# Three blocks with a mixture of experts on one core: expert order from counts, last projection by row tiles, gate vector on expert outputs

## The reference

```python
mod = cond @ w_mod[l] + b_mod[l]
sh1, sc1, g1, sh2, sc2, g2 = [m[:, None, :] for m in jnp.split(mod, 6, axis=-1)]
h = _layer_norm(x) * (1 + sc1) + sh1
y = _token_mixer(h, ..., w_out[l], b_out[l])
x = _layer_norm(DEEPNORM_ALPHA * x + g1 * y, post1_g[l], post1_b[l])
h = _layer_norm(x) * (1 + sc2) + sh2
y = _moe(h, w_router[l], b_router[l], w_gu[l], b_gu[l], w_dn[l], b_dn[l])
x = _layer_norm(DEEPNORM_ALPHA * x + g2 * y, post2_g[l], post2_b[l])
```

## Time and profile before

| | |
|---|---|
| timed runs (3) | 2307.07, 2309.64, 2311.7 us; median 2309.64 |
| profiled execution | 2306.96 us, its span 2304.8 us |
| granted clock of TensorE, mean | 0.985 |
| busy share PE, PEld, DVE, ACT, POOL | 94%, 49%, 33%, 20%, 3% |
| DMA | 591.35 MB, mean 257 GB/s |

### The profile page before, as it was taken

How to read it: one execution, slowest core, us unless ns; L and a number is a source line. 1 busy time by engine, 2 the same in 40 slices (tenths; PEclk the granted TensorE clock), 3 DMA queues, 4 the chain that set the end, 5 groups by cost and what they waited for, 6 DMA issues and landing times.

```text
span 2304.8 us, 30211 instructions
## 1 busy us (share of the span) xinstructions
PE 2159.5 (94%) x11510; PEld 1133.0 (49%) x11511; DVE 752.1 (33%) x1835; ACT 464.1 (20%) x922; POOL 65.4 (3%) x79
## 2 busy tenths in 40 slices
PE   6999999989999998999989998999999999999998
PEld 5744454333333333333333334744565446787873
DVE  1795243222222122222222223231212353988100
ACT  1012111111111111111101111131112215897100
POOL 0000000000000000000000000000000000222000
PEclk9999999999999999999999999999999999999999
DMA  9654667779999999999995899435234333232241
GB/s 375 227 188 147 228 223 279 284 296 418 418 418 417 418 418 383 418 417 418 417 381 223 356 418 354 146 138 190 73 124 146 109 117 112 74 111 74 108 163 40
DMA packets 157319, 591.35 MB, mean 257 GB/s; under 512 B 5072, under 2 KB 5136, under 8 KB 124352
## 3 DMA queue, kind: packets, MB, share of 16 engines
q1 hardware_dynamic: 152240, 572.03, 63.4%
q0 software_dynamic: 4384, 16.40, 2.0%
q10 hardware_dynamic: 624, 1.93, 0.2%
HBM read 589.29 MB, written 1.05 MB: 256 GB/s over the span
## 4 chain that ended last, share of the span: by engine, by line
PE 74%; DMA 15%; DVE 5%; ACT 3%; DVEq 2%; issue 1%; SPq 0%; ACTq 0%
PE PS L609 22%; PE PS L912 14%; DMA W<-in_w_gu 13%; PE PS L597 10%; PE PS L935 6%; PE PS L1119 4%; PE PS L624 4%; PE PS L859 2%; PE PS L948 2%; PE PS L1192 1%; DVE BIG L1875 1%; PE PS L876 1%; DVE BIG L1879 1%; DMA W<-in_w_mod 1%; DVEq L1878 1%
## 5 line engine op out<-in xcount | busy, mean ns | idle before, releaser
L609 PE MATMUL PS<-W,BIG 128*128 128x512 f32 x1152 | 501.4, 596 | 5.0 <-DVE BIG L2309 2.9
L912 PE MATMUL PS<-W,BIG 128*64 128x512 f32 x2048 | 451.8, 595 | 21.2 <-DMA W<-in_w_gu 21.2
L609 PEld LDWEIGHTS PS<-W,BIG 128*128 128x128 f32 x1152 | 219.5, 191 | 277.5 <-issue 270.8
L912 PEld LDWEIGHTS PS<-W,BIG 128*64 128x64 f32 x2048 | 142.1, 137 | 313.2 <-issue 270.9
L935 PE MATMUL PS<-W,BIG 128*64 128x512 f32 x1024 | 228.9, 600 | 6.9 <-ACT BIG L1362 6.9
L597 PE MATMUL PS<-BIG,W 128*128 128x256 f32 x1024 | 222.2, 379 | 1.5 <-ACT BIG L353 1.5
L597 PEld LDWEIGHTS PS<-BIG,W 128*128 128x128 f32 x1024 | 194.2, 190 | 29.0 <-ACT BIG L353 1.9
L1873 DVE TENSOR_SCALAR BIG<-PS 128x512 f32<-128x512 f32 (+1 forms) x38 | 24.7, 650 | 382.2 <-PE PS L912 356.5
L935 PEld LDWEIGHTS PS<-W,BIG 128*64 128x64 f32 x1024 | 71.0, 138 | 143.9 <-issue 126.3
L1119 PE MATMUL PS<-BIG,W 128*128 128x256 f32 x512 | 118.4, 385 | 0.5 <-ACT BIG L1517 0.5
L1357 ACT ACTIVATE BIG<-BIG 128x512 f32<-128x512 f32 x32 | 20.2, 630 | 489.0 <-DVE BIG L1873 489.0
(11 more groups left out here) (452 smaller groups left out, 1942.6 us busy)
## 6 DMA issues: line engine op xcount, KB each, us to landing
W<-in_w_gu SPq DMA_DIRECT2D x128, 2048.0 KB, 17.6
W<-in_w_dn SPq DMA_DIRECT2D x64, 2048.0 KB, 19.2
W<-in_w_in SPq DMA_DIRECT2D x24, 2048.0 KB, 18.9
W<-in_w_mod SPq DMA_DIRECT2D x12, 2048.0 KB, 10.9
W<-in_gla_w_in SPq DMA_DIRECT2D x10, 2048.0 KB, 7.9
W<-in_s_w_in SPq DMA_DIRECT2D x8, 2048.0 KB, 9.0
W<-in_s_w_glu SPq DMA_DIRECT2D x8, 2048.0 KB, 8.6
W<-in_w_out SPq DMA_DIRECT2D x6, 2048.0 KB, 7.7
```

Source lines behind the costliest of these rows:

```text
L609: ins = pe.matmul(ps[:, t, :], lhs(i * KT + k)[:, t * P:(t + 1) * P], w[:, k, :], start=i + k == 0, stop=last_chunk and k == KT - 1)
L912: ins = pe.matmul(PS[hh[h], g, :], XET[:, k, :], gu_w(k)[:, g * D + h * CH:g * D + (h + 1) * CH], start=False, stop=k == KT - 1, skip_grou ...
```

## The change

Four things. (1) The experts are taken in an order worked out on the chip. VectorE ranks them by falling count, with expert 0 set ahead of all and smaller numbers first among equals; the place in the loop of rank r is the number whose five bits are those of r reversed. TensorE brings counts and numbers into that order with two products; `PERM` holds the expert's number for each place. SyncE loads it for the weights' addresses, VectorE at the top of each expert and once more in the branch of the extra blocks. (2) `halves_by_rows` computes row tile 0 of both halves of `w_out`, then tile 1; VectorE adds ALPHA times `X` and g1 times the bias ahead of it, and runs both norms' statistics tile by tile (`tile_scale`), as ScalarE takes the roots. (3) The product with g2 moves to each expert's output: VectorE writes `YE` as the product with `GAIN_H` (`YEX` with `GAIN_Q`) where ScalarE copied it, and `b_dn` is multiplied by g2 once. (4) ALPHA times `X` goes into the PSUM banks by a product with ALPHA times the identity (`residual_in`) in place of the zero sums; behind the loop the statistics are read from PSUM.

```diff
+    own = -np.arange(NE, dtype=np.float32)
+    own[0] = 4 * T * NE
+    c[:, C_TIE:C_TIE + NE] = own
+    c[0:NE, C_OWN] = own
+    c[0:NE, C_OWN + 1] = np.arange(NE)
+    spread = sorted(range(NE), key=lambda i: int(f"{i:05b}"[::-1], 2))
+    c[:, C_PLACE + np.array(spread)] = np.arange(NE)
...
+        def tile_scale(dve, src, t):
+
+            for h in range(2):
+                dve.bn_stats(ST[:, t, 6 * h:6 * h + 6], src[:, t, h * CH:(h + 1) * CH])
+            dve.drain()
+            dve.bn_aggr(MV[:, t, :], ST[:, t, :])
+            dve.drain()
+            dve.tensor_scalar_add(VE[:, t:t + 1], MV[:, t, 1:2], LN_EPS).then_inc(var_ready, 1)
+            norms_in[0] += 1
+            norms_out[0] += 1
+            dve.wait_ge(std_ready, norms_out[0])
+            dve.reciprocal(RS[:, t:t + 1], SD[:, t:t + 1])
...
-                        gu = A["w_gu"][0, bass.ds(e, 1)].rearrange("e (k p) n -> p (e k) n", p=P)
-                        dn = A["w_dn"][0, bass.ds(e, 1)].rearrange("e (k p) n -> p (e k) n", p=P)
+                        source = e if previous is None else sp.value_load(PERM[0:1, bass.ds(e, 1)], min_val=0, max_val=NE - 1)
+                        gu = A["w_gu"][0, bass.ds(source, 1)].rearrange("e (k p) n -> p (e k) n", p=P)
+                        dn = A["w_dn"][0, bass.ds(source, 1)].rearrange("e (k p) n -> p (e k) n", p=P)
...
+        KEY, ABOVE, ORDER = OH[0:NE, 0, :], OH[0:NE, 1, :], LG[0:NE, 0, :]
+        OWN_COUNT, PLACED_COUNT, PLACED_EXPERT = PS[0:NE, 2, 0:1], PS[0:1, 2, NE:2 * NE], PS[0:1, 2, 2 * NE:3 * NE]
...
+                for name in names:
+                    u = UNIT[name][0]
+                    pe.wait_ge(unit_free[u % 2], u // 2)
+                for t in range(TT):
+                    for name in names:
+                        c0 = UNIT[name][3]
+                        if t == 0:
+                            pe.wait_ge(w_landed[slot_no(c0)], load_count(c0))
+                        for k in range(KT):
+                            ins = pe.matmul(unit_ps(name)[:, t, :], lhs(k)[:, t * P:(t + 1) * P], slot(c0)[:, k, :],
+                                            start=k == 0, stop=k == KT - 1)
+                        if t == 1:
+                            ins.then_inc(chunk_done, 1)
+                    if t == 0:
+                        ins.then_inc(ev("first_rows"), 1)
...
+                pe.matmul(OWN_COUNT, SEL[:, t, :], ONES[:, 0:1], start=t == 0, stop=t == TT - 1)
...
-            def zero_sum(q):
-                pe.matmul(PS[:, 4 + q, :], ZW, H2[:, 0, 0:CH], start=True, stop=False, skip_group_check=True)
+            def residual_in(q):
+                for t in range(TT):
+                    pe.matmul(PS[:, 4 + q, t * T:(t + 1) * T], WEIGHTED_ID, X[:, t, q * T:(q + 1) * T],
+                              start=t == 0, stop=False, skip_group_check=True)
...
-                zero_sum(q)
+                residual_in(q)
             gather_rows(0, True)
+            pe.wait_ge(ev("sel_ready"), 2)
+            pe.matmul(PLACED_COUNT, RANK[:, 0:1], ORDER, start=True, stop=True)
+            pe.matmul(PLACED_EXPERT, K[0:NE, C_OWN + 1:C_OWN + 2], ORDER, start=True, stop=True).then_inc(ev("pos_done"), 1)
...
-            keep_active(0, 12)
-            pe.wait_ge(std_ready, 6)
+            keep_active(0, 7)
+            pe.wait_ge(std_ready, 8)
...
+            act_tile_std(act, 0)
+            act_tile_std(act, 0)
+            act_tile_std(act, 1)
             copy_mod("sc2")
-            act_std(act)
...
-                act.wait_ge(ev("down_done"), e + 1)
-                act.activation(YE, PS[:, 2, :], ACT.Copy).then_inc(ev("ye_copied"), 1)
...
-            for i in range(2):
-                rows_from(f"wo{i}", cvr, vec, i)
-            dve.drain()
-            used(dve.tensor_tensor(cvr, cvr, bt(MA), ALU.mult))
-            dve.drain()
+            used(dve.tensor_tensor(cvr[:, 0], MA, vec, ALU.mult))
+            dve.drain()
+            for t in range(TT):
+                dve.scalar_tensor_tensor(X[:, t], X[:, t], ALPHA, cvr[:, 0], ALU.mult, ALU.add)
+            gain, shift = vector(dve, "post1_g"), vector(dve, "post1_b")
+            dve.drain()
+            for t in range(TT):
+                if t == 0:
+                    dve.wait_ge(ev("first_rows"), FIRST_ROWS["wo"])
+                for i in range(2):
+                    name, c = f"wo{i}", slice(i * CH, (i + 1) * CH)
+                    if t == 1:
+                        wait_unit(dve, name)
+                    ins = dve.tensor_tensor(cvr[:, t, c], unit_ps(name)[:, t, :], MA[:, c], ALU.mult)
+                    if t == 1:
+                        free_unit(ins, name)
+                dve.drain()
+                dve.tensor_tensor(X[:, t], X[:, t], cvr[:, t], ALU.add)
+                dve.drain()
+                tile_scale(dve, X, t)
+                dve.scalar_tensor_tensor(X[:, t], X[:, t], MV[:, t, 0:1], gain, ALU.subtract, ALU.mult)
+                dve.drain()
+                dve.scalar_tensor_tensor(X[:, t], X[:, t], RS[:, t:t + 1], shift, ALU.mult, ALU.add)
+                dve.drain()
+                if t == 1:
+                    dve.sem_inc(v_used, 2)
+                    dve.sem_inc(ev("x1_ready"), 1)
+                tile_scale(dve, X, t)
...
-            residual(cvr)
-            full_norm(X, "post1_g", "post1_b", ev("x1_ready"))
-            modulated_norm(H2, X, "sc2", "sh2", ev("rows_ready"))
-            dve.memset(ZW, 0.0)
+            modulate(H2, X, "sc2", "sh2", ev("rows_ready"))
+            dve.tensor_scalar(WEIGHTED_ID, ident, ALPHA, None, ALU.mult)
+            dve.wait_ge(unit_free[UNIT["g2"][0] % 2], UNIT["g2"][0] // 2 + 1)
+            for h in range(2):
+                r = slice(BLK * h, BLK * (h + 1))
+                dve.tensor_copy(GAIN_H[r], MA[r, h * CH:(h + 1) * CH])
+            for q in range(4):
+                r = slice(XBLK * q, XBLK * (q + 1))
+                dve.tensor_copy(GAIN_Q[r], MA[r, q * T:(q + 1) * T])
             dve.wait_ge(ev("moe_small_landed"), 80)
+            dve.tensor_tensor(BDN, BDN, MA[0:NE], ALU.mult)
...
+            def placed(e):
+                return dve.value_load(PERM[0:1, bass.ds(e, 1)], min_val=0, max_val=NE - 1)
...
                 with dve.If(hi - lo > 0):
+                    own = placed(e)
                     with dve.Fori(lo, hi) as x:
-                        extra_block(x, e, nc.s_assert_within(x - lo + 1, 1, XMAX))
+                        extra_block(x, own, nc.s_assert_within(x - lo + 1, 1, XMAX))
...
+                    following = placed(e + 1)
...
+                dve.wait_ge(ev("down_done"), e + 1)
+                dve.tensor_tensor(YE, PS[:, 2, :], GAIN_H, ALU.mult).then_inc(ev("ye_copied"), 1)
...
+            dve.tensor_copy(RANK[:, 0:1], OWN_COUNT)
+            dve.scalar_tensor_tensor(KEY, pos[0:NE, 2, :], float(NE), K[0:NE, C_TIE:C_TIE + NE], ALU.mult, ALU.add)
+            dve.scalar_tensor_tensor(RANK[:, 1:2], OWN_COUNT, float(NE), K[0:NE, C_OWN:C_OWN + 1], ALU.mult, ALU.add)
+            dve.drain()
+            dve.tensor_scalar(ABOVE, KEY, RANK[:, 1:2], None, ALU.is_gt)
+            dve.drain()
+            dve.tensor_tensor_scan(KEY, ONES[0:NE, 0:NE], ABOVE, 0.0, ALU.mult, ALU.add)
+            dve.drain()
+            dve.tensor_scalar(ORDER, K[0:NE, C_PLACE:C_PLACE + NE], KEY[:, NE - 1:NE], None, ALU.is_equal)
+            dve.drain()
+            dve.sem_inc(ev("sel_ready"), 1)
+            dve.wait_ge(ev("pos_done"), 2)
+            dve.tensor_copy(PERM, PLACED_EXPERT)
+            cnt, nx = PLACED_COUNT, TABF[:, 0, :]
...
-            dve.wait_ge(unit_free[UNIT["g2"][0] % 2], UNIT["g2"][0] // 2 + 1)
-            for t in range(TT):
-                dve.tensor_tensor(YOUT[:, t, :].rearrange("p (q n) -> p q n", q=4), PS[:, 4:8, t * T:(t + 1) * T],
-                                  MA.rearrange("p (q n) -> p q n", q=4), ALU.mult)
-            dve.drain()
-            residual(YOUT)
-            full_norm(X, "post2_g", "post2_b", None)
...
+            for t in range(TT):
+                for q in range(4):
+                    dve.bn_stats(HST[:, 4 * t + q, :], PS[:, 4 + q, t * T:(t + 1) * T])
+            dve.drain()
+            for t in range(TT):
+                dve.bn_aggr(MV[:, t, :], HST[:, 4 * t:4 * t + 4, :].rearrange("p q s -> p (q s)"))
+            dve.drain()
+            dve.tensor_scalar_add(VE[:], MV[:, :, 1], LN_EPS).then_inc(var_ready, 1)
+            norms_in[0] += 1
+            root_taken(dve)
+            vec = vector(dve, "post2_g").rearrange("p (q n) -> p q n", q=4)
+            for t in range(TT):
+                ins = dve.scalar_tensor_tensor(X[:, t, :].rearrange("p (q n) -> p q n", q=4), PS[:, 4:8, t * T:(t + 1) * T],
+                                               MV[:, t, 0:1], vec, ALU.subtract, ALU.mult)
+            used(ins)
+            dve.drain()
+            vec = vector(dve, "post2_b")
+            for t in range(TT):
```

(1 more changed line is left out.)

44 lines of the change are left out of this document (28 added, 16 removed).

## The result

Timed in turns on one chip, four runs each: the changed kernel 2285.14 us (2281.91 to 2288.07), the kernel before 2308.36 (2304.79 to 2311.7). The ratio is 0.9896, 95% interval 0.9882 to 0.9910: 23 us faster, where 22.8 had been summed. The profiled execution of the changed kernel took 2286.83 us (span 2285.0, mean granted clock 0.984), 20.1 less than the profiled one of before.

What follows compares the result with a forecast made beforehand. The expert loop, where TensorE and DMA take turns, was the largest part besides projections; plain experts waited for weights. Terms summed to -22.8 from 2306.96, 2284.2; carried to the median 2286.8, stated 2286 us, range 2276 to 2298.

Steps and rivals of the forecast that it cites:

- Expert order: Expert loop: spreading experts with extra blocks cuts plain experts' waits for weights, 17.2 us less; bounds about 9 to 26.4.
- Third load: Branch of heavy experts: VectorE's load of the expert's number adds 0.72 us in each of five, 3.6 more; bounds 0 to 6.
- Expert output on VectorE: Expert loop: VectorE's product in place of ScalarE's copy costs 0 in 31 experts and 0.1 us in the last.
- three low windows of five: Heavy experts: three of five assumed to have granted clock under 1; none or all would shift the time by -5 or +3.
- First block's end: Last projection to logits: tile 0 is normed beneath tile 1, 5.9 us less; bounds 3.6 to 7.5.
- Start of the experts: Ahead of the first expert: own count 0.4 and placing products 0.5, so 0.9 us more; up to 3 if the table is later.
- End of the experts: After the last scatter: residual steps fall away, 4.86 us, PSUM reads add 0.6; 4.3 us less, 3.5 to 4.9.
- the order gains nothing: Rival, 8%, expert loop: something other than extra blocks sets the lead; only the rest counts, -5.6, giving 2304 us.
- a late product: Rival, 3%, every expert: VectorE's gain product is late for the scatter product; 2309.6 us at 1 us over, 2319 at 1.3.
- a loss of the front's gain: Rival, 14%, before the first expert: late table chain or bias load stalls TensorE, takes 4 to 5 us back; 2291 us.
- heavy experts cost double: Rival, 8%, heavy experts: branch code or the free placement of low clock adds 3 to 8 us; 2292 us.
- no heavy expert loses clock: Rival, 7%, heavy experts: no low clock in them, more gain, 2281 to 2275 us.

Runs made afterwards that it cites:

- e1: Changed kernel with its ranking and loads kept, but experts run in order of their numbers: 2302.25 us, ratio 0.9973 to the kernel before.
- e2: Changed kernel with the five experts that have extra blocks at places 1 to 5 in a row: 2324.87 us, ratio 1.0066 to the kernel before.
- e3: Changed kernel with the two-block expert at place 18, other heavy ones at 6, 12, 24 and 30: 2280.27 us, ratio 0.9873.
- e4: Changed kernel with VectorE's load of the expert's own number only at the top of the expert, not in the branch: 2277.39 us, ratio 0.9866.
- e8: Changed kernel with filler products on TensorE before three waits of the extra block: 2279.53 us, ratio 0.9879.
- e10: Changed kernel with the fillers of e8 and the output part undone as in e6: 2283.99 us, ratio 0.9898.
- e6: Changed kernel with ScalarE copying expert output, zero sums, and gate product and residual behind the loop, as before: 2286.81 us, ratio 0.9910.
- e5: Changed kernel with the first block's last projection, gate product, residual and norms on both tiles together, as before: 2286.38 us, ratio 0.9905.
- e12: Changed kernel with e3's places, all three VectorE loads at the top of the expert, and fillers before two waits: 2267.61 us, ratio 0.9820.
- e9: Changed kernel with the fillers of e8 and the front undone as in e5: 2286.02 us, ratio 0.9899.

## Why the prediction was right, point by point

**Expert order, -17.2.** Plain-pace waiting fell from 26.4 to 7.6 us (0.23 + 2.32 + 2.33 at places 14 to 16, 0.32 + 2.35 at 30 and 31): -18.8. The pattern of places was right to 0.2 us each. The lead of 14 us that the prediction reads in the earlier trace rows holds at most for the first chunk, issued at 410.2; the fourth was issued at 422.9 and landed at 432.5 at the earliest. Places 1 to 3 passed all the same, with 83.36 us for the three. The 1.4 allowed for the next stage's transfers at place 31 didn't come: its gate product waits as in place 16. e1 and e2 show that the place is the cause, e3 that three quarters of the remaining waiting goes too.

**Third load, +3.6.** Measured 0.75 a heavy expert in e4, 3.7 in five; e1's expert 16, in the same place as before, is 0.78 longer than in the earlier trace rows. The Trainium skill (DMA: Bandwidth & Descriptors, "Latency and other measured facts") gives `tensor_load` a floor of about 600 ns; here the instruction takes 0.308 us and the whole step 0.75, so it is the step that a plan needs.

**Expert output on VectorE, 0 and +0.1.** No idle time before L1004 in 30 experts, and 0.35 us between the loops of e8 and e10.

**Loop in all.** From the start of expert 1 to the last scatter 1006.19 us became 993.83: -12.4 where -13.5 was summed. -18.8 for waits and +3.7 for loads leave +2.7, and that is clock: its falls cost 7.9 us in the changed kernel's heavy experts (4.6, 1.7 and 1.7) and 4.9 in those of before, and the last expert gives 0.3 back. The prediction took three low windows of five, and three came (0.90, 0.97, 0.97); what it mis-sized is that one of them stayed low three times as long (10.2 us at 1.2 GHz instead of 3.4).

**First block's end, -5.9.** From the last projection's end to the logits 24.3 us instead of 30.5, -6.3. VectorE's second root chain ended 9.6 us after the projection (predicted 9.9), and the shift product waits for its spread, as written. The scale product waits for its own as well, 2.59 us, which was not foreseen and cost nothing, as the shift product waits 4.27 us behind it. The 0.4 beyond the sum may be the clock, 1.00 in this window and 0.89 before; that was not taken apart.

**Start of the experts, +0.9.** Logits to first expert 26.45 us instead of 24.91: +1.5, of which 1.1 is the logits product alone (6.34 instead of 5.26 us; the clock of that window is 0.81). The rows that the change added take 0.22 us (the own count) and 0.21 (the two placing products), half of the 0.9 summed. So the term was too small by 0.6 because the clock was left out, and its own work would have made it too large. The table is done at 365.66, before TensorE has turned the rows (366.30): hidden, as predicted.

**End of the experts, -4.3.** 19.15 us became 14.27, -4.9. Stats over PSUM took 2.75, not 2.9 to 3.2, their aggregation 0.39 instead of 0.28, and the first scaling from PSUM 2.48, no more than from `X`: the surcharge of 0.6 was 0.4. e6 puts 4.5 on this part; the 0.4 beyond it is an idle time of VectorE of 0.47 us with no releaser in the trace of before (ahead of L330), which e6 does not have.

**Sum.** Measured in the two traces: 1.3 more ahead of the change, -6.3, +1.5, +0.2 in expert 0, -12.4, -4.9, +0.6 behind: -20.0, against the -22.8 that were summed from that same trace. The medians say -23.2: the profiled execution of before lay 1.4 under its median, that of after 1.7 over its own. That the medians meet the sum to 0.4 us is therefore luck; the mechanisms are right, and the single terms are off by up to 2.7. How far single executions stray with the clock, the four timed runs show: those of the changed kernel took 2281.91 at 0.988, 2283.45 at 0.986, 2286.83 at 0.984 and 2288.07 at 0.985. The prediction named this term at -5 to +3; the four runs lie 3.2 under and 2.9 over their median. By the Trainium skill (TensorE: Matmul & The Clock Gate, Part 1) the monitor runs free of the kernel and meets it at another phase in each run; four runs of one kernel with clocks from 0.984 to 0.988 agree. But phase alone is not the cause: with the waits filled (e8) it found nothing to slow in the heavy experts.

The rivals: that the order gains nothing is refuted by e1 and e2, a late product by the row of L1004, a loss of the front's gain by the start of expert 0. That heavy experts cost double came half true in the profiled execution, and by clock alone. That no heavy expert loses clock is what e8 brings about, and its 2279.5 us lie in that rival's 2281 to 2275. The second block's first projection (L632) does not wait for weights either: 55.36 us busy of the 55.36 from 1411.20 on.

## What to carry to other kernels

Where a ring of weights holds one unit of work, the stored lead is capped, so what counts is the distance between long units, not their sum: work out how many short ones a lead carries (here 13.5 / 2.33, five) and place the long ones at that distance (the next long one, being the sixth, still waited 0.4 us). Register loads in a branch are paid bare; above it, in a wait that exists anyway, they are free. Before comparing variants a few us apart, compare the clock of their windows, or fill TensorE's short waits first: the times of e5 and e6 could not be read without that.

## What the runs showed of the hardware

- A stretch of 3.4 us at 1.2 GHz inside a heavy expert cost 1.68 us (48.79 at clock 0.97 against 47.11 at 1.00), and 10.2 us of it in place 4 cost 4.6. With fillers the timed runs of e8 spread over 1.8 us and those of e12 over 1.9, where the changed kernel's spread over 6.2; those of e9 and e10, also with fillers, spread over 6.5 and 6.1, so the heavy experts are not the only source.
- `value_load` on VectorE: 0.308 us of instruction, 0.75 us of program.
- Scaling reads PSUM at no surcharge: two 128x1024 scalings in 2.48 us, as from SBUF. Statistics took 2.75 us for eight 128x256 slices of PSUM and 2.47 for four 128x512 slices of SBUF; whether the source or the number of instructions makes the 0.28 is not shown.
- In the last expert, which stands outside the hardware loop, TensorE idles 3.96 us behind the gate product with no releaser that the profile shows ("issue"), 3.37 in e12 and 3.15 in the kernel before. VectorE works for it until 1382.43 (L1969), 2.1 us of the 3.96; what the other 1.85 are was not tried.
